# Cached attention on one core: the sparse value products moved to the array's fourth column group, the inverse sums to the output stage

## What is computed

```python
# stick-breaking, per head: a = beta_k * product of (1 - beta) of later keys
z = einsum('bqhd,bkhd->bhqk', q, k) * 64 ** -0.5
a = where(causal, exp(log_sigmoid(z) + after), 0)
y_b = einsum('bhqk,bkhd->bqhd', a, v) * silu(sg)
# sparse: softmax over the 256 keys that the indexer picks
p = softmax(q_d @ k_d * 64 ** -0.5 over the chosen keys)
y_c = (p @ v_d) * silu(dg)
mix = concat([y_a, y_b, y_c]); x = layer_norm(ALPHA * x + mix @ w_out)
```

## Time and profile before

| | us |
|---|---|
| median of 3 runs | 4616.01 |
| lowest, highest | 4611.08, 4627.89 |
| the profiled execution: its time | 4620.66 |
| its span | 4618.9 |
| TensorE busy in it | 4305.4 |
| VectorE busy | 3457.6 |
| ScalarE busy | 1737.3 |
| GpSimd busy | 1041.7 |

### The profile page before, as it was taken

The page is one execution under the profiler, slowest core; times in us unless marked ns, Lnnn a source line. Parts: engine busy times, 40 slices in busy tenths (PEclk is TensorE's granted clock), DMA queues, the critical chain, the costliest instruction groups (busy, mean ns, idle before and its releaser), DMA issues.

```text
span 4618.9 us, 79623 instructions
## 1 busy us (share of the span) xinstructions
PE 4305.4 (93%) x29678; PEld 2453.3 (53%) x29678; DVE 3457.6 (75%) x5659; ACT 1737.3 (38%) x2538; POOL 1041.7 (23%) x1393
## 2 busy tenths in 40 slices
PE   8987999999899998889999879999999999988899
PEld 6433545754466676454464235457544666765543
DVE  2685999999799764554537859999997997646445
ACT  3553212211177776330035522122112767854300
POOL 4220035500034332110042101354000433411100
PEclk9998999999999999999999989999999999999999
DMA  2102210211232003884211022102112320049832
GB/s 79 33 15 63 66 24 29 77 53 51 77 112 78 27 29 122 279 282 161 93 48 32 17 66 59 24 31 79 52 52 78 114 72 27 29 129 302 269 113 91
DMA packets 343763, 396.99 MB, mean 86 GB/s; under 512 B 100311, under 2 KB 264242, under 8 KB 340050
## 3 DMA queue, kind: packets, MB, share of 16 engines
q1 hardware_dynamic: 318034, 375.10, 25.8%
q10 hardware_dynamic: 25344, 16.79, 1.3%
HBM read 297.71 MB, written 94.14 MB: 85 GB/s over the span
## 4 chain that ended last, share of the span: by engine, by line
PE 78%; ACT 5%; issue 5%; DVE 4%; DMA 3%; SPq 2%; ACTq 1%; POOL 1%; DVEq 0%; POOLq 0%
PE banks L884 20%; PE banks L887 13%; PE banks L2127 10%; PE banks L328 5%; PE banks L368 4%; PE banks L1529 3%; PE banks L1211 3%; PE banks L1499 3%; PE banks L1249 3%; PE banks L1513 2%; PE banks L1233 2%; DVE arena L1362 2%; PE banks L1823 1%; PE banks L1828 1%; PE banks L1839 1%
## 5 line engine op out<-in xcount | busy, mean ns | idle before, releaser
L1037 DVE TENSOR_SCALAR_CACHE_REDUCE arena<-arena 128x1920 uint8<-128x1920 f32 (+13 forms) x896 | 1259.0, 1473 | 0.0
L884 PE MATMUL banks<-arena 128*128 128x512 f32 x2176 | 937.4, 592 | 0.0
L884 PEld LDWEIGHTS banks<-arena 128*128 128x128 f32 x2176 | 409.9, 189 | 520.4 <-issue 520.4
L887 PE MATMUL banks<-arena 128*128 128x384 f32 (+1 forms) x2048 | 620.0, 459 | 2.4 <-POOLq L142 2.4
L1362 DVE TENSOR_TENSOR_SCAN arena<-arena 128x129 f32<-128x129 f32 (+3 forms) x480 | 535.4, 1175 | 29.3 <-ACT arena L1273 18.4
L467 DVE SCALAR_TENSOR_TENSOR arena<-arena 128x512 f32<-128x512 f32 (+3 forms) x532 | 403.7, 759 | 118.7 <-ACT arena L433 69.0
L887 PEld LDWEIGHTS banks<-arena 128*128 128x128 f32 x2048 | 380.1, 189 | 207.3 <-POOLq L142 2.6
L2127 PE MATMUL banks<-arena 128*128 128x512 f32 x1024 | 443.9, 596 | 13.2 <-DMA arena<-in_w_out 13.2
L1594 DVE CUSTOM_DVE_ANT_0 arena<-banks,arena 128x512 f32<-128x512 f32 (+3 forms) x480 | 269.5, 607 | 159.4 <-PE banks L1499 158.9
L433 ACT ACTIVATE arena<-banks 128x1024 f32<-128x1024 f32 (+3 forms) x304 | 278.5, 919 | 243.3 <-PE banks L368 136.9
L368 PE MATMUL banks<-arena 64*128 64x512 f32 (+3 forms) x1216 | 308.3, 594 | 60.4 <-ACT arena L433 59.0
(11 more groups left out here) (201 smaller groups left out, 5431.8 us busy)
## 6 DMA issues: line engine op xcount, KB each, us to landing
arena<-in_cache_sb_kv SPq DMA_DIRECT2D x256, 384.0 KB, 4.2
arena<-in_cache_dsa_kv SPq DMA_DIRECT2D x144, 128.0 KB, 4.3
arena<-in_x_prompt SPq DMA_DIRECT2D x32, 512.0 KB, 4.3
arena<-mixT SPq DMA_DIRECT2D x32, 512.0 KB, 4.0
arena<-xs SPq DMA_DIRECT2D x32, 512.0 KB, 4.4
arena<-in_cache_dsa_kv ACTq DMA_DIRECT2D x112, 128.0 KB, 4.5
arena<-in_w_in SPq DMA_DIRECT2D x8, 1536.0 KB, 7.5
out<-arena SPq DMA_DIRECT2D x64, 192.0 KB, 1.9
```

The source lines that it names most:

```text
L884: m = nc.tensor.matmul(bank[i % 4][:, :], W2[c % 2][:, k, j * P:(j + 1) * P], xT[:, k, t * FREE:(t + 1) * FREE], start=(k == 0), stop=(k = ...
L887: m = nc.tensor.matmul(bank[i % 4][:, 0:WD[name]], xT[:, k, t * P:(t + 1) * P], W2[c % 2][:, k, 0:WD[name]], start=(k == 0), stop=(k == KC ...
L1037: nc.vector.tensor_scalar(dummy[j % 2][:, 0:v.shape[-1]], v, thr[:, t:t + 1], 0.0, ALU.is_ge, ALU.add, accum_out=history[:, k, t:t + 1]).t ...
```

## The change

The sparse value product of a page tile becomes two matmuls, one for each key/value head, with 24 weights (3 heads of 8 queries) by 64 columns; both write partitions 96 to 119, the fourth column group, which the stick rows leave free. Both kinds now lie in columns 0 to 127 of bank 7 and are evacuated into one buffer, the sparse rows by a plain copy of 24 rows. The sums of all sequences are kept, inverted once at the end of the stage, stored to DRAM as 48 x 8 numbers and read back by token in eight small DMAs in tile 2 of the output stage; there GpSimd multiplies the sparse gates by them, one instruction more, before the other products. Counts of semaphores follow.

```diff
@@ sattn_tensor: values
-                if m < NAU:
-                    b, c = unit(m)
-                    for jj in range(APC if c else 1):
+                c = m % ACH
+                rows = slice(0, P if c else NS)
+                for jj in range(APC if c else 1):
+                    last = c == ACH - 1 and jj == APC - 1
+                    if m < NAU:
                         for p in range(3):
                             r = slice(32 * p, 32 * p + QROWS[p])
                             a = jj * SROWS + 32 * p
-                            rows = slice(0, P if c else NS)
                             v = asb[chunk(m) % NASB][:, jj, 384 + p * P:384 + (p + 1) * P] if c else anew[:, 384 + p * P:384 + (p + 1) * P]
                             k = nc.tensor.matmul(bank[7][r, 0:P], awp[m % 2][rows, a:a + QROWS[p]], v,
-                                                 start=(c == 0), stop=(c == ACH - 1 and jj == APC - 1), skip_group_check=True)
-                if m >= ACH:
-                    b, c = unit(m - ACH)
-                    for jj in range(APC if c else 1):
-                        a = APC * SROWS + jj * DROWS
-                        rows = slice(0, P if c else NS)
-                        v = ada[chunk(m - ACH) % NADA][:, jj, P:2 * P] if c else anew[:, 896:1024]
-                        k = nc.tensor.matmul(bank[7][0:DROWS, P:2 * P], awp[m % 2][rows, a:a + DROWS], v,
-                                             start=(c == 0 and m >= NAU), stop=(c == ACH - 1 and jj == APC - 1), skip_group_check=True)
+                                                 start=(c == 0), stop=last, skip_group_check=True)
+                    if m >= ACH:
+                        for g in range(2):
+                            a = APC * SROWS + jj * DROWS + g * 24
+                            e = g * HD
+                            v = ada[chunk(m - ACH) % NADA][:, jj, P + e:P + e + HD] if c else anew[:, 896 + e:896 + e + HD]
+                            k = nc.tensor.matmul(bank[7][96:120, e:e + HD], awp[m % 2][rows, a:a + 24], v,
+                                                 start=(c == 0 and g == 0), stop=last, skip_group_check=True, tile_position=(0, 96))
@@ sattn_scalar
-                                         accum_out=ars[r % 2][0:DROWS]).then_inc(s_aex, 1)
+                                         accum_out=ars[0:DROWS, r:r + 1]).then_inc(s_aex, 1)
@@ sattn_vector
                     if i:
-                        dve.wait_ge(s_amx, at(s_amx, 3 * (l * NB + i)))
-                        nc.vector.tensor_scalar(ayc[0:DROWS, i - 1, :], bank[7][0:DROWS, P:2 * P], ari[(i - 1) % 2][0:DROWS], None, ALU.mult).then_inc(s_aye, 1)
-                if s >= ACH + 2 and (s - 2) % ACH == 0 and (s - 2) // ACH <= NB:
-                    r = (s - 2) // ACH - 1
-                    dve.wait_ge(s_aex, at(s_aex, l * NB + r + 1))
-                    dve.wait_ge(s_aye, at(s_aye, l * 2 * NB + max(0, 2 * r - 2)))
-                    nc.vector.reciprocal(ari[r % 2][0:DROWS], ars[r % 2][0:DROWS]).then_inc(s_amx, 1)
+                        nc.vector.tensor_copy(ayb[96:120, i - 1, :], bank[7][96:120, 0:P]).then_inc(s_aye, 1)
+            dve.wait_ge(s_aex, at(s_aex, (l + 1) * NB))
+            nc.vector.reciprocal(ari[0:DROWS, :], ars[0:DROWS, :]).then_inc(s_aye, 1)
@@ new function
+        def store_inverse_sums(sp):
+            sp.dma_start(ISD, ari[0:DROWS, :]).then_inc(s_ays, 16)
@@ output_sync
+            store_inverse_sums(sp)
             for h in range(HSB):
                 store_y(sp, h)
...
                     sp.dma_start(oy[0:NS, :], YS[:, :]).then_inc(s_ol, 16)
+                    for b in range(NB):
+                        sp.dma_start(ois[b * NQ:(b + 1) * NQ, :], ISD[:, b:b + 1].rearrange("(h q) o -> q (h o)", q=NQ),
+                                     allow_slow_non_contiguous=True).then_inc(s_ol, 16)
@@ output_gpsimd
-            pool.wait_ge(s_ol, at(s_ol, 128 * (l + 1)))
+            pool.wait_ge(s_ol, at(s_ol, 256 * (l + 1)))
+            og6 = og[r, 384:768].rearrange("p (h d) -> p h d", h=HDSA)
+            nc.gpsimd.tensor_tensor(og6, og6, ois[r].unsqueeze(2).broadcast_to([NS, HDSA, HD]), ALU.mult).then_inc(s_omix, 1)
```

More of the change, by code:

```diff
@@ L81, in build @@
     YTD = nc.dram_tensor("mixT", (D, SEQ), F32).ap()
+    ISD = nc.dram_tensor("sample_inverse_sums", (HDSA * NQ, NB), F32).ap()
     SBD = nc.dram_tensor("sample_bias", (NB * HDSA * NQ, NKEY), F32).ap()
@@ L411, in index_scalar @@
             if l:
-                act.wait_ge(s_omix, at(s_omix, 7 * l))
+                act.wait_ge(s_omix, at(s_omix, 8 * l))
             take_x(0)
@@ L1633, in build @@
         awn, apn = carve(NS), carve(NS)
-        amx, anm, ars, ari = ([carve(k) for _ in range(2)] for k in (8, 1, 1, 1))
-        assert W_AT + 4 * SEQ // 2 + 6 * FREE >= W_AT + 2 * NKEY + 4 * CW4 + CW4 + 4 * NS + 2 * NS + 22
+        amx, anm = ([carve(k) for _ in range(2)] for k in (8, 1))
+        ars, ari = carve(NB), carve(NB)
+        assert W_AT + 4 * SEQ // 2 + 6 * FREE >= W_AT + 2 * NKEY + 4 * CW4 + CW4 + 4 * NS + 2 * NS + 34
         A_DK = W_AT + 2 * SEQ + 6 * FREE
@@ L1643, in build @@
         adqT = carve(NB * DROWS).rearrange("p (b r) -> p b r", b=NB)
-        ayb, ayc = (carve(NB * P).rearrange("p (b c) -> p b c", b=NB) for _ in range(2))
+        ayb = carve(NB * P).rearrange("p (b c) -> p b c", b=NB)
         A_NEW = ARENA - 1024
-        assert A_DK + 5 * APC * 256 + 4 * APC * 768 + 4 * (FREE + 1) + 3 * CW4 + NB * (SROWS + DROWS) + 2 * NB * P <= A_NEW
+        assert A_DK + 5 * APC * 256 + 4 * APC * 768 + 4 * (FREE + 1) + 3 * CW4 + NB * (SROWS + DROWS) + NB * P <= A_NEW
         anew = arena[0:NS, A_NEW:ARENA]
@@ L1734, in store_y @@
             a, r = h % 2 * HD, 32 * (h // 2) + h % 2 * NQ
-            g = h // 3 * HD
+            g, d = h // 3 * HD, 96 + h % 3 * NQ
             sp.dma_start(YS[:, h * HD:(h + 1) * HD].rearrange("(b q) d -> q b d", q=NQ), ayb[r:r + NQ, :, a:a + HD]).then_inc(s_ays, 16)
-            sp.dma_start(YS[:, 384 + h * HD:384 + (h + 1) * HD].rearrange("(b q) d -> q b d", q=NQ), ayc[h * NQ:(h + 1) * NQ, :, g:g + HD]).then_inc(s_ays, 16)
+            sp.dma_start(YS[:, 384 + h * HD:384 + (h + 1) * HD].rearrange("(b q) d -> q b d", q=NQ), ayb[d:d + NQ, :, g:g + HD]).then_inc(s_ays, 16)
+        def store_inverse_sums(sp):
+            sp.dma_start(ISD, ari[0:DROWS, :]).then_inc(s_ays, 16)
         def sattn_sync(sp, l):
@@ L1958, in sattn_vector @@
                         nc.vector.reduce_max(anm[b % 2][0:DROWS], amx[b % 2][0:DROWS, 0:ACH], AX_X).then_inc(s_amx, 1)
-                        dve.wait_ge(s_amx, at(s_amx, 3 * (l * NB + b) + 1))
+                        dve.wait_ge(s_amx, at(s_amx, 2 * (l * NB + b) + 1))
                         nc.vector.tensor_scalar(anm[b % 2][0:DROWS], anm[b % 2][0:DROWS], -1.0, None, ALU.mult).then_inc(s_amx, 1)
@@ L2012, in build @@
         mix, ocv = carve(D), carve(768)
+        ois = carve(HDSA)
         ost, omv, ove, ors, otm = carve(12), carve(2), carve(1), carve(1), carve(1)
@@ L2056, in output_sync @@
             load_output_second(sp, l)
-            sp.wait_ge(s_aye, at(s_aye, 2 * NB * (l + 1)))
+            sp.wait_ge(s_aye, at(s_aye, (2 * NB + 1) * (l + 1)))
+            store_inverse_sums(sp)
             for h in range(HSB):
@@ L2098, in output_gpsimd @@
             nc.gpsimd.tensor_tensor(ocv[r], ou[r], cw[r], ALU.mult).then_inc(s_omix, 1)
-            pool.wait_ge(s_omix, at(s_omix, 7 * l + 4))
+            pool.wait_ge(s_omix, at(s_omix, 8 * l + 5))
             nc.gpsimd.tensor_tensor(ocv[r, 0:256], ocv[r, 0:256], ocv[r, 256:512], ALU.add).then_inc(s_omix, 1)
-            pool.wait_ge(s_omix, at(s_omix, 7 * l + 5))
+            pool.wait_ge(s_omix, at(s_omix, 8 * l + 6))
             nc.gpsimd.tensor_tensor(ocv[r, 0:256], ocv[r, 0:256], ocv[r, 512:768], ALU.add).then_inc(s_omix, 1)
-            pool.wait_ge(s_omix, at(s_omix, 7 * l + 6))
+            pool.wait_ge(s_omix, at(s_omix, 8 * l + 7))
             nc.gpsimd.tensor_tensor(mix[r, 0:256], ocv[r, 0:256], obg[r], ALU.mult).then_inc(s_omix, 1)
@@ L2110, in output_tensor @@
                 if t == NT - 1:
-                    pe.wait_ge(s_omix, at(s_omix, 7 * (l + 1)))
+                    pe.wait_ge(s_omix, at(s_omix, 8 * (l + 1)))
                     for j in range(2):
```

7 lines of the change are left out of this document (4 added, 3 removed).

## The result

| | us |
|---|---|
| before, median of 20 runs | 4620.82 (4610.23 to 4627.89) |
| changed, median of 20 runs | 4626.31 (4618.74 to 4633.64) |
| ratio, with its 95% interval | 1.0015 (1.0009 to 1.0022) |
| the profiled execution of the changed kernel | 4624.24, span 4622.5 |

The change makes the kernel slower by 5.5 us, with 37 us less of work on TensorE. The forecast was 3.5 us less than before. (The first three of these 20 runs of before are the ones whose median, 4616.01, the forecast of 4612 started from.)

A forecast was written before the change was run, and what follows sets the result against it. TensorE, page transfers and a dependence ring were candidate bounds in one attention stretch. From 4620.66, less 4.9 gained, plus 1.4 for the clock: 4617.2, or 4612 against the median; range 4598 to 4630.

The forecast's parts named there:

- step c=0: A sequence's new-rows step, under ScalarE's chain; no gain forecast, its TensorE idle growing by 0.8 us to 2.5.
- one fall more: One more drop of TensorE's granted clock to 1.2 GHz after idle, in the whole run; cost 1.4 us.
- step c=4: A sequence's fourth page-unit step, under ScalarE's chain from sigmoid to next logits; no gain forecast.
- c=1: A sequence's first page-unit step, full value products of both kinds; at most 0.47 us gained, 5.68 to 5.2 us.
- rival 3: With 0.8 us more idle, the clock falls in step c=0 of nearly every sequence; 4625 us, chance 0.16.
- Values of a unit with both kinds: Stick and sparse value products of a full page unit: 1.2 us instead of 2.0, giving back 0.8.
- issue bound of 38 ns a record: Value products' issue time, taken from the key transposes: 40 records make 1.5 us.
- Rival 2: Fourth column group doesn't run beside the others; 4616 us at half price, 4658 at full; chance 0.13.
- ring: Attention's dependence loop: logits, ScalarE's sigmoid, VectorE's scan and key copy, next logits; limits the first page-unit step's gain to 0.47 us.
- half pass: Attention stretch at DMA share 1.00: transfers let half of five 0.47 us gains through, 1.2 us a layer.
- The end of the stage: Last value product, and so the output weights' load behind it, comes 0.8 us sooner per layer.
- both my bounds: Issue of the eight small DMAs in the output stage: 0.64 or 3.99 us each; counted as nothing.

The follow-up runs named there:

- after_again: The changed kernel as it is, run again beside the others on the same chip; 4625.3 us, ratio 1.0012 to the kernel before.
- hold: Changed kernel with the output stage's second group of loads issued only once the output weights have landed; 4626.2 us, ratio 1.0012.
- tail_only: Changed kernel with 36 idle identity products at the start of the output stage alone; 4621.4 us, ratio 0.9997.
- output_part: Kernel before with only the change's second half: sums kept, inverted once, read back in eight small DMAs; sparse products as they were; 4623.9 us, ratio 1.0004.
- before_tail: Kernel before with 24 idle identity products at the start of the output stage; 4611.4 us, ratio 0.9979.
- light runs: Stick pages from a layer's ninth chunk on bring only keys: kernel before 1.0004, changed kernel 1.0016, changed kernel with idle products 0.9990.
- pad_tail: Changed kernel with four idle products at the ends of steps c=4 and c=0 and 36 at the output stage's start; 4610.5 us, ratio 0.9982.
- pad_4_8: Changed kernel with four idle identity products at the end of step c=4 and eight at the end of step c=0; 4618.6 us, ratio 0.9998.

## Why the prediction was wrong

**The step that failed is the clock's.** It said that the idle of step c=0 grows "by 0.8 us, to 2.5" and counted one fall more, +1.4 us. The idle grew to 3.66, from 1.71 in the same place, and there were eight falls more, +10.3 us in the two profiles. The sigmoid of step c=4 starts a chain of ScalarE that no value product enters, as the prediction itself said; so both value products under it, that of step c=4 and that of c=0, turn into idle ahead of the same logits, and I had counted one. Where no page wait lies in the chain (sequence 2 of either layer), from the logits of c=4 to those of c=1 it is 10.7 us before and after, and the idle in it went from 1.86 to 3.67, twice 0.9. The condition of rival 3, "nearly every sequence", was then met: ten falls.

A second reading failed beside it. The forecast rested on "2.38 us of idle fell, 1.71 did not", from layer 0 alone. The fall at 4334.07, behind 1.85 us, was in the same trace; steps behind 1.86 to 1.89 us kept full clock. So one layer's six places were no count for the run, and the length of the idle no sure sign.

The rival forecast 4625; it had 0.16 and should have been the forecast. Its place and its price (1.4 us; 6.54 in the mean of the ten against 5.20, so 1.3) were right. That it comes so near to 4626.3 is in part luck: it had ten falls more, eight were measured, it gained 4.9 us, where the shorter steps c=1 alone gave back 5.6, and it had nothing for the output stage.

The account of the profiles, mean of the plain changed ones against the plain ones of before: the stretch is 155.9 us (changed, after_again, hold, tail_only) against 153.1 (before, output_part, before_tail), +2.8 a layer. Steps c=1 alone make it: the twelve of a run take 77.7 us in the mean of the same changed ones against 71.1, +6.6, where the two stretches together grow by 5.5. The output stage from its first to its last prompt product is 222.9 (changed, after_again, hold) against 222.2 (before, output_part), +0.7. Twice 3.5 is 7.0 us, against 5.5 measured and 6.9 by the ratio. In all 20 runs of the changed kernel the mean granted clock lies between 0.968 and 0.972; in the 35 runs of the kernel before beside after_again it lies between 0.973 and 0.977. The falls are no accident of one profile.

Point by point:
- Values of a unit with both kinds: 1.2 us taken, 1.0 measured; 24 and 16 records lie in 2024.33 to 2025.4. The issue bound of 38 ns a record was no bound: 40 records went in 1.04 us, 26 ns each. Rival 2 is out. The fourth group cost nothing here: 1.04 us with it, 1.00 for the stick products alone before. The Trainium skill's figure for three column tiles, 2.38 times ("TensorE: Matmul & The Clock Gate", Part 3), is under what this array did.
- Step c=1 at full clock: forecast 5.2, measured 5.20 in both steps that had it. The ring is right.
- The transfers' floor: the term "half pass" rested on a DMA share of 1.00 as a bound. The light runs show none for either plain kernel beyond their intervals. The waits of the key transposes for sparse pages did grow as forecast, from 3.5 to 6.1 us in the stretch. A full queue and a stretch of time that match each other are no proof that one sets the other.
- The end of the stage: 0.8 us sooner, forecast. From the last unit's logits to the first output product it is 25.3 us in the mean before and 25.4 changed: the gain is gone in a load longer by 1 us in the mean, for a reason that stays open and may be chance.
- The output stage's clock was not in the prediction at all. TensorE is idle 9.45 us ahead of it in layer 0, and its first products run at the low clock for longer: 5.4 us in the mean of six stages (changed, after_again, hold) against 3.9 in four (before, output_part). tail_only shows what this place is worth.
- Eight small DMAs: 0.36 us each, under both my bounds, and hidden.
- VectorE, GpSimd: nothing, as said.

## To carry to other kernels

Where an engine's clock depends on its being busy, time taken off it ahead of a wait is not neutral: add up every saving between the start of the other engine's chain and its end, and look at the idle that results, before counting the saving as nothing. If that idle stands ahead of work on the critical path, fill it with products that nobody reads, or put real work there; here that turned 1.0012 into 0.9980. Stop the filling where the wait ends: in pad_tail it outlasted the load by over 2 us. Ask the same of the kernel as it is: 24 idle products ahead of its output stage, with no other change, gave 0.9979, as much as the change with both repairs.

## What the runs showed of the hardware

- The time of a run goes with its mean granted clock: within the 12 runs of pad_4_8, from 4612.19 us at 0.977 to 4628.28 at 0.974, with a correlation of -0.94. The runs without a profile don't show where the clock was low; in the profiled one it was in no step c=1.
- Idle before the logits and their clock: full after 1.71, 1.75 and 1.86 us, and also in two cases after 3.29 and 3.22 us of the changed kernel, where the fall came a little later, within the same step (6.24 and 6.28 us); half after 1.85, 2.38 and 3.66. The idle's length does not decide alone. Of the changed kernel's two steps c=1 at full clock, one had its idle in two pieces, 2.06 and 1.75 us with transposes at full clock between them. In the other the clock had fallen in step c=0 already, behind 1.03 us of idle (transposes in 1.90 us), and was back for the logits.
- TensorE's timeline in the last units of the changed kernel, below, shows the sparse halves alone: 16 records in 1.08 us, as long as 8 whole ones before. Beside the stick products they are free (24 and 16 records in 1.04 us). What pays is the neighbour, not the smaller tile.

```profile
2062.60 1.08 PE L1892 MATMUL banks<-arena 128*24 128x64 f32 x16
```
